# A transformer stack in fp32: compression weights read where they land, and a new order of the NSA turns

## The reference, cut to what matters

```python
def compress(t, pos_emb, w1, b1, w2):
    ...
    flat = jnp.moveaxis(blocks, 3, 2).reshape(b, -1, g, CMP_BLOCK * d)
    return jax.nn.gelu(flat @ w1 + b1) @ w2

def token_mixer(...):
    k_cmp = compress(kv[:, :, 0], cmp_pos_k, ck_w1, ck_b1, ck_w2)
    v_cmp = compress(kv[:, :, 1], cmp_pos_v, cv_w1, cv_b1, cv_w2)
    ...
    y_nsa = nsa_attention(q, q_rot, k_cmp, v_cmp, k_slc, v_slc, k_win, v_win, gates)
    ...
    g_conv, g_nsa, g_mem = jnp.split(jax.nn.sigmoid(merge_g), 3, axis=-1)
```

## Time and profile before

| | us |
|---|---|
| median of 3 runs (range) | 1727.38 (1727.22 to 1727.48) |
| the profiled execution: time | 1727.93 |
| the profiled execution: span | 1726.1 |
| TensorE busy | 1718.0 (100%) |
| VectorE busy | 1073.1 (62%) |
| ScalarE busy | 917.9 (53%) |
| mean granted TensorE clock | 0.999 |

### The profile page before, as it was taken

The page is one execution under the profiler, slowest core; times in us unless marked ns, Lnnn a source line. Parts: engine busy times, 40 slices in busy tenths (PEclk is TensorE's granted clock), DMA queues, the critical chain, the costliest instruction groups (busy, mean ns, idle before and its releaser), DMA issues. The chain is left out here.

```text
span 1726.1 us, 31112 instructions
## 1 busy us (share of the span) xinstructions
PE 1718.0 (100%) x12536; PEld 1586.6 (92%) x12536; DVE 1073.1 (62%) x1523; ACT 917.9 (53%) x1258; POOL 35.0 (2%) x60
## 2 busy tenths in 40 slices
PE   9999999999999999999999999999999999999998
PEld 9999888999999999999998999899999889989997
DVE  6555787655655566556677555755584557775555
ACT  6444677444454445567746444644464577664443
POOL 0000120000000000000000000000000000000000
PEclk9999999999999999999999999999999999999999
DMA  9655534655665555453355555655555553446552
GB/s 328 249 193 193 185 110 151 228 184 194 224 227 188 184 193 207 171 220 126 144 198 194 193 188 199 231 203 193 190 206 189 178 193 125 171 160 229 185 194 95
DMA packets 48415, 328.58 MB, mean 190 GB/s; under 512 B 5584, under 2 KB 5840, under 8 KB 10192
## 3 DMA queue, kind: packets, MB, share of 16 engines
q1 hardware_dynamic: 45504, 316.93, 51.0%
q10 hardware_dynamic: 2832, 10.54, 1.7%
HBM read 326.39 MB, written 1.05 MB: 190 GB/s over the span
## 5 line engine op out<-in xcount | busy, mean ns | idle before, releaser
L1262 DVE TENSOR_TENSOR lo<-raw,hi 128x2048 fp32r<-128x2048 f32 x267 | 611.2, 2292 | 307.3 <-ACT hi L710 306.9
L710 ACT ACTIVATE hi<-raw 128x2048 fp32r<-128x2048 f32 x267 | 511.1, 1915 | 373.7 <-PE work L1891 343.7
L1889 PE MATMUL work<-xT_hi,hi 128*128 128x256 f32 x2464 | 685.7, 278 | 0.0
L1890 PE MATMUL work<-xT_lo,hi 128*128 128x256 f32 x2464 | 681.1, 276 | 0.0
L1891 PE MATMUL work<-xT_hi,lo 128*128 128x256 f32 x2464 | 681.0, 276 | 0.0
L1889 PEld LDWEIGHTS work<-xT_hi,hi 128*128 128x128 f32 x2464 | 462.7, 188 | 4.3 <-issue 1.7
L1890 PEld LDWEIGHTS work<-xT_lo,hi 128*128 128x128 f32 x2464 | 463.0, 188 | 2.4
L1891 PEld LDWEIGHTS work<-xT_hi,lo 128*128 128x128 f32 x2464 | 462.8, 188 | 0.0
L1891 PE MATMUL acc<-hi,hT_lo 128*128 128x512 f32 x480 | 189.1, 394 | 0.0
L1890 PE MATMUL acc<-lo,hT_hi 128*128 128x512 f32 x480 | 188.3, 392 | 0.0
L1889 PE MATMUL acc<-hi,hT_hi 128*128 128x512 f32 x480 | 186.5, 389 | 0.0
(11 more groups left out here) (357 smaller groups left out, 2108.7 us busy)
## 6 DMA issues: line engine op xcount, KB each, us to landing
raw<-stream SPq DMA_DIRECT2D x295, 1024.0 KB, 4.8
mem_in<-mem ACTq DMA_DIRECT2D x3, 1024.0 KB, 5.1
post<-post ACTq DMA_DIRECT2D x6, 512.0 KB, 3.9
raw<-stream SPq DMA_DIRECT2D x4, 512.0 KB, 8.7
memT_raw<-mem2T ACTq DMA_DIRECT2D x2, 1024.0 KB, 7.2
xT_raw<-xT SPq DMA_DIRECT2D x4, 256.0 KB, 5.4
raw<-stream SPq DMA_DIRECT2D x4, 256.0 KB, 5.6
x<-x SPq DMA_DIRECT2D x2, 512.0 KB, 8.7
```

The lines of the kernel that those rows point to most:

```text
L710: nc.scalar.activation(dst, raw[:, s, :], ACT.Copy).then_inc(hi_ready, 1)
L1262: nc.vector.tensor_tensor(lo[:, s, :], raw[:, s, :], hi[:, s, :].bitcast(F32), ALU.subtract).then_inc(lo_ready, 1)
L1889: nc.tensor.matmul(dst, a_hi, b_hi, start=start, stop=False)
L1890: nc.tensor.matmul(dst, a_hi, b_lo, start=False, stop=False)
```

## The change

Compression units are no longer copied: TensorE reads them from `raw` as soon as they have landed. Hence the load that overwrites such a unit waits for TensorE's use instead of lo_ready, the next split unit counts for three on hi_ready and lo_ready, and SyncE's loop is written out between units 54 and 58. In the NSA part, gelu of the value half is moved ahead; in pair 0 compressed_out comes after 5 steps, the first turn and the scores of slots 4 and 5 after 12, the second turn after 22 (before: 13, 13 and 18, 23); in pairs 1 to 3 both turns come together after 20 steps (before: after 13 and 23).

```diff
-NSA_PLAN = {0: (13, 18, 23), 1: (13, 23, 23), 2: (13, 23, 23), 3: (13, 23, 23)}
+FIRST_PLAN = (5, 12, 22)
+TURN_AT = 20
...
-        whole = place("whole", [P, RING, UNIT], r_hi)
...
+        def steps_of(sec, n):
+
+            return 3 if exact(sec, n - 1) and exact(sec, n - 2) else 1
...
         def _(sp):
+            whole_units = [Section(layer).unit(n) for layer in range(LAYERS) for n in L_EXACT]
+
             def load(n, trip=0):
 
-                wait(sp, lo_ready, n - RING + 1 + trip * RING)
+                if n - RING in whole_units:
+                    sp.wait_ge(unit_used, n - RING + 1)
+                else:
+                    wait(sp, lo_ready, n - RING + 1 + trip * RING)
...
+                cut = base + L_CMP[0] + RING
+                turns = (cut - at) // RING
+                load_turns(at, at + RING * turns)
+                for n in range(at + RING * turns, base + L_CMP[1] + RING + 2):
+                    load(n)
+                at = base + L_CMP[1] + RING + 2
...
             def split_high(sec, n, trip=0):
 
+                if exact(sec, n):
+                    return
...
-                dst = (whole if exact(sec, n) else hi)[:, s, :]
-                nc.scalar.activation(dst, raw[:, s, :], ACT.Copy).then_inc(hi_ready, 1)
+                nc.scalar.activation(hi[:, s, :], raw[:, s, :], ACT.Copy).then_inc(hi_ready, steps_of(sec, n))
...
                 for n in pair_of(0):
                     high_tile(sec, n, jobs[n])
+                hid_tanh(1)
                 merge_out(3)
...
                     for n in range(first, first + 4):
+                        if t == 0 and n == first + 2:
+                            step_work("kcvc", 0)
                         exps(sec, n, jobs[n])
                     if t == 0:
-                        hid_tanh(1)
-                        step_work("kcvc", 0)
-                    else:
-                        for n in range(first + 4, first + 6):
-                            exps(sec, n, jobs[n])
-                    for slot in range(2):
+                        for slot in range(2):
+                            copy_nsa(sec, t, slot, T + P)
+                    for n in range(first + 4, first + 6):
+                        exps(sec, n, jobs[n])
+                    merge_high(4 + 2 * t)
+                    for slot in range(2 if t == 0 else 0, 2):
                         copy_nsa(sec, t, slot, T + P)
-                    if t == 0:
-                        for n in range(first + 4, first + 6):
-                            exps(sec, n, jobs[n])
-                    merge_high(4 + 2 * t)
...
             def split_low(sec, n, trip=0):
                 s = sec.slot(n)
+                if exact(sec, n):
+                    return
                 dve.wait_ge(hi_ready, sec.unit(n + 1) + trip * RING)
-                if exact(sec, n):
-                    k = len(L_EXACT) * sec.layer + L_EXACT.index(n)
-                    nc.vector.memset(passed[:, k:k + 1], 0.0).then_inc(lo_ready, 1)
-                    return
...
+                hid_cube(1)
                 for n in pair_of(0):
                     low_tile(sec, jobs[n])
+                hid_gated(1)
...
                         for n in pair_of(1):
                             low_tile(sec, jobs[n])
-                        hid_cube(1)
                     for n in range(first, first + 2):
                         normalise(sec, n, jobs[n])
-                    if t == 0:
-                        hid_gated(1)
...
                         n, pairs = L_CMP[c] + half, CMP_PAIRS // 2
-                        parts_ready(sec, n)
+                        pe.wait_ge(landed[sec.slot(n)], sec.landed(n))
...
-                                                    whole[:, sec.slot(n), CMP_HIDDEN * q:CMP_HIDDEN * (q + 1)],
+                                                    raw[:, sec.slot(n), CMP_HIDDEN * q:CMP_HIDDEN * (q + 1)],
...
                 for t in range(NSA_HEADS // 2):
-                    cut = NSA_PLAN[t]
                     for b in range(2 if t == 0 else 3):
                         scores(sec, 2 + 3 * t + b, jobs)
-                    merged_steps(t, 0, cut[0])
                     if t == 0:
+                        merged_steps(0, 0, FIRST_PLAN[0])
                         compressed_out()
-                    turn_nsa(sec, t, 0, jobs)
-                    merged_steps(t, cut[0], cut[1])
-                    if t == 0:
+                        merged_steps(0, FIRST_PLAN[0], FIRST_PLAN[1])
+                        turn_nsa(sec, 0, 0, jobs)
                         pe.wait_ge(evac_done, sec.fill(F_KCVC + 1))
                         pe.wait_ge(scored, sec.at(2 * JOBS[0], 2 * JOBS[1], 2 * (4 + 4)))
                         scores(sec, 4, jobs)
-                    merged_steps(t, cut[1], cut[2])
-                    turn_nsa(sec, t, 1, jobs)
-                    merged_steps(t, cut[2], 4 * KD)
+                        merged_steps(0, FIRST_PLAN[1], FIRST_PLAN[2])
+                        turn_nsa(sec, 0, 1, jobs)
+                        merged_steps(0, FIRST_PLAN[2], 4 * KD)
+                    else:
+                        merged_steps(t, 0, TURN_AT)
+                        turn_nsa(sec, t, 0, jobs)
+                        turn_nsa(sec, t, 1, jobs)
+                        merged_steps(t, TURN_AT, 4 * KD)
                     values_nsa(sec, t, jobs)
```

More of the change, by code:

```diff
@@ L717, in high_piece @@
                     act.wait_ge(landed[s], sec.landed(n))
-                nc.scalar.activation(hi[:, s, begin:end], raw[:, s, begin:end], ACT.Copy).then_inc(hi_ready if end == UNIT else hi_piece, 1)
+                nc.scalar.activation(hi[:, s, begin:end], raw[:, s, begin:end], ACT.Copy).then_inc(
+                    hi_ready if end == UNIT else hi_piece, steps_of(sec, n) if end == UNIT else 1)
             def load_post(sec, r):
@@ L1256, in split_low @@
                 s = sec.slot(n)
+                if exact(sec, n):
+                    return
                 dve.wait_ge(hi_ready, sec.unit(n + 1) + trip * RING)
-                if exact(sec, n):
-                    k = len(L_EXACT) * sec.layer + L_EXACT.index(n)
-                    nc.vector.memset(passed[:, k:k + 1], 0.0).then_inc(lo_ready, 1)
-                    return
-                nc.vector.tensor_tensor(lo[:, s, :], raw[:, s, :], hi[:, s, :].bitcast(F32), ALU.subtract).then_inc(lo_ready, 1)
+                nc.vector.tensor_tensor(lo[:, s, :], raw[:, s, :], hi[:, s, :].bitcast(F32),
+                                        ALU.subtract).then_inc(lo_ready, steps_of(sec, n))
             def low_piece(sec, n, begin, end, count):
@@ L1272, in low_piece @@
                 if end == UNIT:
-                    ins.then_inc(lo_ready, 1)
+                    ins.then_inc(lo_ready, steps_of(sec, n))
             def ask_root(c, parts, eps):
```

## The result

The changed kernel takes **1739.45 us** (median of six, 1738.25 to 1745.5) against 1728.18 us for six executions of the kernel before (1727.22 to 1729.51): a ratio of **1.0069 [1.0058, 1.0079]**, 11.3 us slower. The forecast was 1733.8 with a range up to 1737.5. So the sign and the place were right, and the price was too low.

A forecast was written before the change was run, and what follows sets the result against it. TensorE, working 1718.0 of 1726.1 us, bounds the kernel. Late loads cost 3.7 us a layer less 0.9 gained, +5.6 for both; 0.8 for instruction fetches makes +6.4 on median 1727.4: 1733.8 us, range 1729.5 to 1737.5.

The forecast's parts named there:

- Gelu's second half, first pair: TensorE's waits on hid (0.38 us) and the first pair's probabilities (0.51 us) go: -0.9 us a layer.
- Joined turns: Pairs 1 to 3, both turns in one place: 0, bounds -0.1 to +0.1 us for each of six pairs.
- Rival D: Joined turns wait for a late last normalise: with 0.5 us each, +3 us more, 1737 us; chance 6%.
- The copies that go: Eight ScalarE copies of 1.9 us and eight VectorE memsets lie beside TensorE, so removing them is worth 0.
- Step 1: Loading queue: u54 waits for TensorE's use of u51; u54, u55, u56 issued at 758.7, 759.6, 760.0.
- Step 2: Landings at 422 GB/s, 2.5 us apart: u54 at 763.5, u55 at 766.0, u56 at 768.5; u54 on time.
- Step 3: ScalarE's split of u56, 2.45 us later, delays merge 1's copy; TensorE stands 2.1 us before the value compression.
- about one in five: Chance that an instruction fetch delays a load; four deciding loads, 0.8 us added, bounds 0 and 6 us.
- Steps 4 and 5: u57's late load delays its split and low part: TensorE waits 0.9 us before rot 3, 0.7 before merge 3.
- Step 6: u56's low part is done at 772.7, needed after 772.9; u58 and u59 land before 793: nothing more.
- Rival C: Pauses drop TensorE's granted clock from 2.4 to 1.2 GHz, 2 us a layer: 1738 us; chance 7%.
- second half: The part of the load chain through u57: waits before rot 3 (0.9 us) and merge 3 (0.7 us) a layer.

The follow-up runs named there:

- e1_order: The kernel before with only the new order of gelu and the turns; copies and loads unchanged: 1725.87 us, 0.9984 [0.9975, 0.9993].
- e7_first: The kernel before with gelu sooner and the first pair's new plan, old turns in pairs 1 to 3: 1726.53 us, 0.9986 [0.9977, 0.9995].
- e8_join: The kernel before with only the joined turns of pairs 1 to 3, after 20 steps: 1728.78 us, 0.9999 [0.9990, 1.0008].
- e5_late: The kernel before, ScalarE copies kept, only the loads of units 54, 55, 57, 58 waiting for TensorE's use: 1738.8 us, 1.0053 [1.0038, 1.0069].
- e2_raw: The kernel before in its old order, with compression units read from raw and the late loads: 1739.69 us, 1.0075 [1.0055, 1.0095].
- e6_copies: The changed kernel with ScalarE's split of u56 moved behind the copies of merge 1, rot 1 and hid 0: 1735.16 us, 1.0040 [1.0025, 1.0056].
- e3_swap: The changed kernel with the load of u56 issued ahead of that of u55: 1731.55 us, 1.0015 [1.0006, 1.0024].

## Why the prediction was right and where it failed

- *Gelu's second half, first pair: -0.9 us a layer.* Right: both waits are gone (waits after, and of e1_order); e7_first measured -2.4 us for both layers (0.9 to 4.0 by the interval) where the term was -1.8, and by its trace TensorE gains 1.1 us over the first pair of each layer where 0.9 was given.
- *Joined turns: 0.* Right: e8_join 0.9999 [0.9990, 1.0008], and between the traces the three pairs of a layer differ by 0.04 us. Rival D has no row: no turn of pairs 1 to 3 waits.
- *The copies that go: 0.* In agreement, not isolated: e5_late, with the copies, has 1.0053 [1.0038, 1.0069], e2_raw, without them, 1.0075 [1.0055, 1.0095]. That TensorE reads `raw` as fast as `whole` is shown (1.87 and 1.86 us).
- *Step 1.* Right: issues at 758.47, 759.34, 759.71, where 758.7, 759.6, 760.0 were given.
- *Step 2, the first step that failed.* u54 landed at 763.19 and u55 at 765.68, as computed (763.5, 766.0). u56 landed at 769.44 instead of 768.5, and since the layer ran 0.17 us early, that is 1.1 us off. The gap to the load ahead was 3.76 us where 2.5 were put. The stretch shows it: the DMA moves 433 GB/s and then 139.

```profile
764.00:766.50 2.50, 2.50 (x25) 2.50 (x24) 0.00 (x0) 0.00 (x0) 0.00 (x0) 1.00 1.02 433
766.50:769.50 3.00, 2.28 (x14) 1.72 (x11) 0.00 (x0) 0.00 (x0) 0.00 (x0) 1.00 0.35 139
```

The DMA queues of 766.5 to 768.0 have one packet beside the load's, of an instruction fetch (queue, packets, MB, share of 16 engines). 4.2% of 16 engines over 1.5 us is 1.0 us of one engine, which the load's share on that engine would have to wait for:

```profile
q1 hardware_dynamic: 63, 0.39, 64.4%
q8 instruction: 1, 0.02, 4.2%
```

  A load lands in 16 parts. Of u56, 15 were in by 768.15 and the last at 769.44, and after 768.0 the load moved only two packets (the same view for 768.0 to 769.5): one of the sixteen parts was behind the others.

```profile
q1 hardware_dynamic: 2, 0.01, 1.3%
```

  I had put "about one in five" for such a meeting. In the six kernels with late loads there are twelve bursts of u54, u55, u56. In ten of them a fetch falls inside and one gap is 3.7 to 4.0 us (10.97 to 11.34 us from the issue of u54 to the landing of the last of the three); in one no fetch falls inside, in one it comes only 0.3 us before the last landing, and both gaps are 2.4 to 2.6 (9.76 and 9.72 us). One in five was counted for single loads of 5 us; the wrong thing was to use it for a burst of 10 to 11 us. (Nor does 0.8 us follow from it: four loads, one in five, 1.5 us each make 1.2.) The gaps and the one late part go together with the fetch in ten bursts of ten, but no run moved or removed the fetches, so the cause is likely, not shown. The Trainium skill (Runtime: NRT & Kernel Launch, "Instruction fetch mechanics") says that a sequencer fetches blocks of 16 KB through a DMA queue of its own and that the cost is mostly hidden; the trace has the packet (0.02 MB), and here its cost would be on the path.
- *Step 3, the chain behind the split.* The mechanism is right, and e6_copies and e3_swap prove it from two sides. The size follows step 2: pauses of 3.3 and 3.4 us, start to start, where 2.1 was given.
- *Steps 4 and 5.* Right in kind; 1.6 us were given for the two. In layer 0 they are 0.5 for rot 3 and 0.8 for merge 3, 1.3 together; in layer 1 they are 1.5 and 0.8, 2.3 together, since u57 landed 6.2 us after its issue where 4.7 were put. Step 6 is right: nothing more waits.
- *Rival C, the clock, 7%, the second step that failed.* The sum has no term for it. This failed most, and it is rather a term of the sum than a rival: it came on top of the forecast's mechanism, in both layers, with 1.33 and 1.59 us. I argued from the earlier trace rows that a pause of 2.1 us was safe, and the pause was 3.3. One pause in one trace was no bound either: in layer 0 of e5_late the clock fell though no wait around it was longer than 1.06 us. The price I gave (2 us each) was somewhat high. The Trainium skill's warning (TensorE: Matmul & The Clock Gate, "HAM oscillation") is what this trace shows: a wait for DMA, and the burst behind it at 1.2 GHz. I had left it at a chance, with nothing in the sum for a pause that comes out longer than forecast.

The sum by spans, from the starts of the same matmuls in both kernels: layer 0 loses 6.0 us, layer 1 7.3, the order gives back 2.2, and the rest of the program ran 0.7 us shorter in this execution. That is the 10.4 us. Against the forecast of +6.4: pauses 2.6 more, clock 2.9 more, second half 0.3 more, the allowance of 0.8 for fetches already counted in these, the order 0.4 less, the rest 0.7 less: +10.3. The way from there to 1739.45 has two parts. The kernel before has a median of 1728.18 in this comparison instead of 1727.38, and the medians are 11.3 us apart where the two profiled executions are 10.3 apart.

Open is what makes the clock fall. e2_raw paused 3.33 us in layer 0 and its clock fell; in layer 1 it paused longer, and the stretch 1402 to 1406 shows 1.00:

```profile
1403.31 1.93 PE L2395 MATMUL work<-raw,cmp_x 128*32 128x256 f32 x32 [3.64 <-issue]
```

In e6_copies pauses of 2.8 and 2.9 us left it at 1.00 in the profile, while two of its other three executions have a mean clock of 0.998 against 0.999. In e5_late it fell behind waits of at most 1.06 us. So the length of one pause alone doesn't decide, and these runs don't show what does. That e2_raw, with one fall instead of two in its profile, is no faster by its median than the whole change is no riddle: its two layers lose 2.8 us less than those of the changed kernel, it lacks the order's 2 us, and the spans (1736.1 and 1736.5) differ by 0.4.

## What to carry to other kernels

A slot that its reader frees instead of a copy moves the next load behind the reader. Count that load's landing, with the loads queued behind it as one burst, and follow not only who reads the unit but everything that stands behind its split on the same engine. When a forecast ends with a pause of the main engine, put a term for the clock into the sum, with its chance, even where the pause looks short; filling the pause with idle matmuls can be cheaper than leaving it (2.9 us by the medians here). A chance meeting has to be counted for the whole burst that it can fall into: one in five for a load was ten in twelve for the burst here.

## What the runs showed of the hardware

- Of three queued 1 MB loads the first lands 4.7 to 4.9 us after its issue and the others 2.5 us apart when undisturbed, at 433 GB/s; in ten bursts with an instruction fetch of 16 KB inside, one gap is 3.7 to 4.0 us, and of the load behind it one of 16 parts comes more than a microsecond after the others.
- Behind pauses of 3.3 and 3.4 us the granted clock fell in both layers of the changed kernel, and the compression took 3.2 and 3.5 us instead of 1.86. It fell in one layer of e2_raw behind 3.33 us and not in the other behind 3.64 us, and in e5_late (0.72 in 780 to 784) behind waits of at most 1.06 us. With TensorE kept busy over the same stretch it was 1.00 in the profile and in three of four executions by the mean, and the program was 2.4 us shorter by its span.
- Two turns in one place instead of two cost and gave nothing that could be told: 0.9999 [0.9990, 1.0008] for six pairs.
